# Hybrid decoder block: stick-breaking attention rebuilt around a scan from PSUM, weighing on POOL, and a transposed output

## The reference

```python
logits = q @ k.T * 64 ** -0.5
mask = key_pos[None, :] < q_pos[:, None]
log_1m_beta = where(mask, log_sigmoid(-logits), 0)
after = reverse_cumsum(log_1m_beta) - log_1m_beta
w = where(mask, exp(log_sigmoid(logits) + after), 0)
out = w @ v
```

## Time and profile before

| | us |
|---|---|
| Median of 3 runs | 3464.99 |
| All runs | 3459.66 to 3466.51 |
| Span of the profiled execution | 3462.9 |

### The profile page before, as it was taken

How to read it: one execution, slowest core, us unless ns; L and a number is a source line. 1 busy time by engine, 2 the same in 40 slices (tenths; PEclk the granted TensorE clock), 3 DMA queues, 4 the chain that set the end, 5 groups by cost and what they waited for, 6 DMA issues and landing times. The chain is left out here.

```text
span 3462.9 us, 45834 instructions
## 1 busy us (share of the span) xinstructions
PE 3115.5 (90%) x16210; PEld 2630.0 (76%) x16210; DVE 1877.4 (54%) x2584; ACT 1109.0 (32%) x1924; POOL 406.0 (12%) x245
## 2 busy tenths in 40 slices
PE   6999909978888896997699979999999899999998
PEld 5888807768778785886588758888888788888887
DVE  4332266579889896342666544444444544444444
ACT  4333205445555555231344321111111121111110
POOL 1221237612122121100000000000000000000000
PEclk9999959989999998998799989999999999999999
DMA  5233251062232203232422251111111311111111
GB/s 163 78 85 94 65 68 33 26 164 50 52 88 59 51 7 80 85 109 86 145 69 90 80 194 49 48 48 48 48 48 47 148 61 48 48 48 48 48 36 61
DMA packets 244273, 251.76 MB, mean 73 GB/s; under 512 B 123520, under 2 KB 197248, under 8 KB 244096
## 3 DMA queue, kind: packets, MB, share of 16 engines
q1 hardware_dynamic: 244112, 249.74, 24.7%
HBM read 189.79 MB, written 58.73 MB: 72 GB/s over the span
## 5 line engine op out<-in xcount | busy, mean ns | idle before, releaser
L2478 DVE TENSOR_TENSOR f_y<-f_ps_down,f_y 128x1024 f32<-128x1024 f32 x256 | 313.2, 1224 | 324.8 <-PE f_ps_down L2588 324.8
L2421 ACT ACTIVATE f_act_f<-f_ps_up 128x512 f32<-128x512 f32 x128 | 76.5, 598 | 1031.6 <-PE f_ps_up L2572 1031.6
L2570 PE MATMUL f_ps_up<-f_ht_hi,f_up_hi 128*128 128x512 f32 x1024 | 401.0, 392 | 6.4 <-DVE f_act_f L2495 6.4
L2586 PE MATMUL f_ps_down<-f_down_hi,f_a_hi 128*128 128x512 f32 x1024 | 400.5, 391 | 6.1 <-issue 6.1
L2571 PE MATMUL f_ps_up<-f_ht_lo,f_up_hi 128*128 128x512 f32 x1024 | 400.3, 391 | 0.0
L2572 PE MATMUL f_ps_up<-f_ht_hi,f_up_lo 128*128 128x512 f32 x1024 | 400.1, 391 | 0.0
L2588 PE MATMUL f_ps_down<-f_down_hi,f_a_lo 128*128 128x512 f32 x1024 | 400.1, 391 | 0.0
L2587 PE MATMUL f_ps_down<-f_down_lo,f_a_hi 128*128 128x512 f32 x1024 | 399.9, 390 | 0.0
L2495 DVE SCALAR_TENSOR_TENSOR f_act_f<-f_ps_up,f_act_f 128x512 f32<-128x512 f32 x128 | 88.5, 691 | 394.9 <-ACT f_act_f L2421 394.9
L823 PE MATMUL a_ps_y<-a_v,a_wt 128*128 128x64 f32 x2176 | 275.9, 277 | 0.0
L823 PEld LDWEIGHTS a_ps_y<-a_v,a_wt 128*128 128x128 f32 x2176 | 267.8, 196 | 1.7
(11 more groups left out here) (317 smaller groups left out, 5925.1 us busy)
## 6 DMA issues: line engine op xcount, KB each, us to landing
f_up_raw<-in_w_up SPq DMA_DIRECT2D x32, 1024.0 KB, 5.4
f_down_raw<-in_w_down SPq DMA_DIRECT2D x32, 1024.0 KB
p_xt<-in_x SPq DMA_DIRECT2D x16, 512.0 KB, 4.8
q<-p_qt SPq DMA_DIRECT2D x16, 512.0 KB, 3.2
k<-p_qt SPq DMA_DIRECT2D x16, 512.0 KB, 3.2
a_q<-q SPq DMA_DIRECT2D x16, 512.0 KB, 9.1
a_k_hi<-k SPq DMA_DIRECT2D x32, 256.0 KB, 5.7
a_k_lo<-k SPq DMA_DIRECT2D x32, 256.0 KB, 6.8
```

Source lines behind the costliest of these rows:

```text
L2478: dve.tensor_tensor(y[:, t, :], down_ps[t % 2][:, :], y[:, t, :], ALU.add).then_inc(added.sem, 1)
L2570: pe.matmul(o, up_hi[:, k, cols], ht_hi[:, k, rows], start=(k == 0), stop=False)
L2586: pe.matmul(o, a_hi[par][:, s, rows], down_hi[:, s, cols], start=(s == 0), stop=False)
```

## The change

- A step now interleaves its two heads: slots alternate between them, each head has its own `left` pair, and all 192 slots are written out with no loop; semaphores count straight through.
- ACT writes `on` first (to SBUF), then sigmoid(-z) in place in PSUM. DVE scans from PSUM, with a broadcast column of ones as the second operand. `off` is gone. A score now waits for the scan of the slot two before it.
- POOL weighs all slots.
- The copies of the transposed groups are shared so that every third group is DVE's, the others ACT's.
- The order: PE does turn(m - 2), gather(m - 6) for both heads at every second slot, score(m + 2); ACT the sigmoids of m, then the copies of m - 4; DVE scan(m), copies of m - 4, output copy of m - 8. There are three `on` and `w` and four `wt` buffers; `z_ps`, `wt_ps` and `y_ps` stay at two each.
- The gather has `v` stationary (64 columns) and `wt` moving (128 columns): head 0 writes partitions 0 to 63 of `y_ps`, head 1 the other half, so the output is transposed (`y_sb` becomes 512 x 2048) and is stored in rows of channels.
- Queries, keys and values come in halves of 1024 positions, keys and values with three buffers. A score piece ends at the half's edge.
- In `mix_heads` the transposes of `ys` are gone; `ys` and its squares live in the freed weight buffers. ACT squares and rounds all four tiles of a step, POOL adds the four tiles of squares of both halves together (four additions a step), and PE sums with 8 products instead of 16. `sums` and `norms` move from the end of a step to the start of the next, behind the first product.

The core of the diff:

```diff
+    SLOTS = [(s, a, *u) for s in range(STEPS) for u in UNITS for a in range(2)]
+    ONS, WS, WTS = 3, 3, 4
+    TURN_LAG, COPY_LAG, GATHER_LAG, Y_LAG = 2, 4, 6, 8
-        by_act = [g[1] > 0 or g[0] % 3 == 0 for g in groups]
+        by_act = [g % 3 != 2 for g in range(len(groups))]
...
+            def sigmoids(m):
+                z = z_ps[m % 2][:, 0:k1 - k0]
+                act.wait_ge(scored, m + 1)
+                if m >= ONS:
+                    act.wait_ge(weighed, m - ONS + 1)
+                act.activation(on[m % ONS][:, 0:k1 - k0], z, ACT.Sigmoid, scale=SCALE).then_inc(sig_on, 1)
+                act.activation(z, z, ACT.Sigmoid, scale=-SCALE).then_inc(sig_off, 1)
...
+            for m in range(N + COPY_LAG):
+                if m < N:
+                    sigmoids(m)
+                if m >= COPY_LAG:
+                    copies(m - COPY_LAG)
...
+                dve.tensor_tensor_scan(left[a][i % 2][:, at + k0:at + k1][:, ::-1], z_ps[m % 2][:, 0:k1 - k0][:, ::-1],
+                                       one[:, 0:1].to_broadcast([P, k1 - k0]),
+                                       1.0 if first else left[a][i % 2][:, at + k1:at + k1 + 1],
+                                       ALU.mult, ALU.bypass).then_inc(scanned, 1)
...
+            for m in range(N + Y_LAG):
+                if m < N:
+                    scan(m)
+                if COPY_LAG <= m < N + COPY_LAG:
+                    copies(m - COPY_LAG)
+                if m >= Y_LAG and m % 2 == 0:
+                    copy_y(m - Y_LAG)
...
+            def score(m):
+                if m >= 2:
+                    pe.wait_ge(scanned, m - 1)
...
+            def turn(m):
+                pe.wait_ge(weighed, m + 1)
+                for g in range(first_group[m], first_group[m + 1]):
+                    if g >= 2:
+                        wait_copied(pe, g - 2)
...
+            def gather(m):
+                wait_copied(pe, first_group[m + 2] - 1)
+                for t in range(tiles):
+                    for a in range(2):
+                        mm = pe.matmul(y_ps[i % 2][a * HEAD:(a + 1) * HEAD, 0:P], v[a][(2 * s + half) % 3][:, row, :],
+                                       wt[(m + a) % WTS][:, t, :], start=(first and t == 0), stop=(last and t == tiles - 1))
...
+            for m in range(N + GATHER_LAG):
+                if TURN_LAG <= m < N + TURN_LAG:
+                    turn(m - TURN_LAG)
+                if m >= GATHER_LAG and m % 2 == 0:
+                    gather(m - GATHER_LAG)
+                if m + 2 < N:
+                    score(m + 2)
...
+                pool.wait_ge(y2_squared.sem, y2_squared.at(c, NF))
+                pool.tensor_tensor(y2_sq[:, 0:2, :], y2_sq[:, 0:2, :], y2_sq[:, 2:4, :], ALU.add).then_inc(folded.sem, 1)
+                pool.wait_ge(ys_squared.sem, ys_squared.at(c, NF))
+                pool.tensor_tensor(ys_sq[:, 0:2, :], ys_sq[:, 0:2, :], ys_sq[:, 2:4, :], ALU.add).then_inc(folded.sem, 1)
...
-            def turn(c, j, count):
-                for k in range(4):
-                    mm = pe.transpose(turn_ps[:, k, :], ys[:, j, k * P:(k + 1) * P], ident[:, :])
```

More of the change, by code:

```diff
@@ L630, in wait_copied @@
[L630 to L645, removed]
+        q_loaded = [sem(f"q_loaded{h}") for h in range(2)]
@@ L647, in _, with wait, wait_copied, load_half @@
+        block = ctx.enter_context(nc.Block())
+        def wait(eng, of, count):
+            if count > 0:
+                eng.wait_ge(of, count)
+        def wait_copied(eng, g):
+            wait(eng, copied_a, acts_before[g + 1])
+            wait(eng, copied_d, g + 1 - acts_before[g + 1])
         @block.sync
         def _(sp):
[L649 to L653, removed]
+            def load_half(s, half):
+                cols = slice(half * HALF, (half + 1) * HALF)
+                r = (2 * s + half) % 3
@@ L717, in copies @@
                         _, t0, n = groups[g]
[L718 to L728 removed]
+                        act.wait_ge(turned, g + 1)
@@ L771, in _ @@
-            with dve.Fori(0, STEPS) as s:
-                for m in range(N + 4):
-                    if m < N:
-                        scan(s, m)
-                    if 1 <= m <= N and not by_pool[m - 1]:
-                        weigh(dve, s, m - 1, weighed)
-                    if 2 <= m < N + 2:
-                        copies(s, m - 2)
-                    if m >= 4:
-                        copy_y(s, m - 4)
+                    dve.wait_ge(gathered, m // 2 + 1)
+                    if s > 0:
+                        dve.wait_ge(y_stored[i // (BLOCKS // 2)], s * DMA)
@@ L802, in score @@
+                    mm = pe.matmul(out, q2[a][:, i * P:(i + 1) * P], k2_lo[a][r][:, cols], start=False, stop=closes and not diagonal)
                     if diagonal:
@@ L827, in _ @@
-            with pe.Fori(0, STEPS) as s:
-                score(s, 0)
-                score(s, 1)
-                for m in range(N + 3):
-                    if m + 2 < N:
-                        score(s, m + 2)
-                    if m >= 3:
-                        gather(s, m - 3)
-                    if 1 <= m <= N:
-                        turn(s, m - 1)
+                    mm.then_inc(turned, 1)
+            def gather(m):
+                s, _, i, k0, k1, first, last = SLOTS[m]
+                wait_copied(pe, first_group[m + 2] - 1)
+                if first:
+                    half = i // (BLOCKS // 2)
+                    if i in (0, BLOCKS // 2):
+                        pe.wait_ge(v_loaded[half], (s + 1) * 2 * DMA)
+                    wait(pe, y_copied, blocks_of[m] - 1)
+                tiles = (k1 - k0) // P
+                for t in range(tiles):
+                    tile = k0 // P + t
+                    half, row = tile // (BLOCKS // 2), tile % (BLOCKS // 2)
+                    for a in range(2):
+                        mm = pe.matmul(y_ps[i % 2][a * HEAD:(a + 1) * HEAD, 0:P], v[a][(2 * s + half) % 3][:, row, :],
+                                       wt[(m + a) % WTS][:, t, :], start=(first and t == 0), stop=(last and t == tiles - 1))
+                mm.then_inc(gathered, 1)
@@ L1443, in _ @@
                 first.load_weights(sp, n, w_loaded[n % RAW])
-            for j in range(TILES):
-                load_ys(0, j)
+            load_ys(0)
             load_uy(1)
```

380 lines of the change are left out of this document (172 added, 208 removed).

## The result

| | before | after |
|---|---|---|
| Median, us | 3464.3 (4 runs) | 4044.7 (4 runs) |
| All runs | 3459.7 to 3466.5 | 4041.3 to 4050.6 |
| Ratio, 95% interval | | 1.168 [1.166, 1.170] |
| Attention in the profiled execution | 697 to 1343 | 697 to 1932 |
| From attention's end to the last instruction | 2120 | 2116 |

The forecast was 4130 with a range of 3930 to 4310, and rival 3 (the two heads' gathers side by side) said 4045. Attention takes 1235 us instead of 646, and nothing else changed by more than 4 us.

What follows compares the result with a forecast made beforehand. Attention was taken as throughput-bound, DVE first, until the new order makes PE's score wait on older copies: 3463 + 684 (attention) - 17 (mixing) = 4130, 4132 with 2 us to the median, given as 4130; range 3930 to 4310, own range 4030 to 4230.

Steps and rivals of the forecast that it cites:

- rival 3: Attention's gather: two heads' products run side by side in PE's array, 0.06 us per record; total 4045 us; chance 0.16.
- What bounded before, and the engines' gains: Attention: throughput binds, DVE first; DVE falls from 561 to about 400 us, POOL gets 394, ACT stays near 400.
- The wait that the new order makes: PE's queue: score(m + 2) waits for slot m + 1's sigmoids and DVE-group scan; none ahead for 160 of 192 slots.
- One turn: Attention's chain from score to next score: 6.63 us mean, 7.8 with the clock, for each of 160 slots.
- The gather: PE in attention: 0.09 us per record, since the load is half as wide; 1.13 us per slot, ends 0.76 and 1.47.
- The clock: PE in attention: idle gaps lower the granted clock, half the work at each level, adding 1.2 us per turn.
- Mixing: After attention: fewer transposes and sums on PE, about 1 us of POOL's additions showing; -17 us, bounds -25 and +10.
- 1: PE's clock in attention stays high despite the idle gaps; total 3943 us; chance 0.13.
- 2: PE's clock in attention stays low nearly throughout; total 4338 us; chance 0.13.
- 4: Attention: transposes do not hold the score, the two `z_ps` tiles bind at 2.5 us a slot; total 3286; chance 0.05.
- What would show it: Attention's profile: PE, DVE, ACT each under half busy, hardly any overlap, clock near 0.7; wrong if attention under 1000 us.
- -160 us: Attention: what it would lose from DVE's lighter work if throughput still bound; the new order was to prevent it.

Runs made afterwards that it cites:

- e1: Changed kernel with PE's order score(m+2), gather(m-6), turn(m-2) instead of turn, gather, score: 3357.1 us, ratio 0.970 to the kernel before.
- e2: Changed kernel, its order on PE kept, with copies 3 slots behind instead of 4: 3458.5 us (1 run).
- e4: Changed kernel with the gather's loops exchanged, all tiles of head 0 and then of head 1: 4115.6 us (1 run).
- e6: Changed kernel with PE's order score, gather, turn and the gather's loops exchanged, one head after the other: 3396.8 us, ratio 0.980 to the kernel before.
- e10: Kernel before with scan from PSUM, all weighing on POOL, copies 3 slots behind instead of 2, gather 4 instead of 3: 3451.6 us, ratio 0.995.
- e13: Kernel before with scan from PSUM, all weighing on POOL, later copies and gather, and output copied 6 slots behind instead of 5: 3454.4 us, ratio 0.996.
- e9: Kernel before with only POOL weighing every slot, the scan still reading SBUF: 3485.8 us (1 run).
- e8: Kernel before, old order, with only the second sigmoid kept in PSUM for the scan and POOL weighing every slot: 3532.8 us, ratio 1.020.

## Why the prediction was right

**What bounded before, and the engines' gains.** DVE 390 us of attention (about 400 forecast), scans 324 (319), ACT 372 (near 400): right. POOL 283, not 394: I scaled its 2.05 us of the earlier trace rows, measured beside scans that read SBUF; 768 columns take 1.55, apart from any scan in the changed kernel and beside scans from PSUM in e1. That nothing of this shows in the time was right, for the reason given.

**The wait that the new order makes.** Shown, by e1 and e2 against the changed kernel: place and lag of the score cost 688 us, more than the 589 by which attention grew, since the other parts gain about 100 once the ring is open. The count of slots was the step that carried the prediction. One detail of it is off: a slot of exactly four tiles has one group, and each head has two such slots (one is half of the nine-tile block), so 152 slots have two groups and 40 have one, not 160 and 32. From scan to scan the changed kernel's trace gives the 152 slots 1028 us, 6.8 each, and the small ones, priced at 2 us, 165 us, 4.2 each. So the turn was overestimated by more, and the small slots underestimated, than the division below shows; it keeps the forecast's counts, to be laid beside its terms.

**One turn.** With the forecast's 64 + 12 + 5 us for small slots and ends, the measured turn is (1235 - 81) / 160 = 7.2 us; forecast 7.8. Term by term:

- Sigmoids (0.81 + 0.81 for 768 columns) and scan (1.76 to 1.82 for 768): as forecast. The sigmoid of 768 columns that writes PSUM takes 0.81 us, as much as the one that writes SBUF.
- ACT's end to the scan: forecast 0.28 from one row, measured 1000.02 + 1.02 to 1001.07, 0.03, which is also the median of all 192. For the two thirds of slots with a DVE group: -27 us.
- The gather: forecast 0.09 at the high clock, 0.129 with my clock; measured 0.107. On 160 x 6.3 x 4 / 2 = 2016 records -45 us. This is the term that was mis-sized most. Its mechanism was wrong too: the forecast let a narrower load make every record faster, and e4 and e6 show that the pairing of the two heads does (unpaired, e6's products start every 0.109 us, against 0.112 in the kernel before, whose load is twice as wide). e4, without the pairing, takes 4116 against my 4130, but that is no confirmation: its record takes 338.3 / 2176 = 0.155 us, not 0.129.
- The clock: half at each level would be 0.75, "near 0.7" was written, measured 0.65. The factor between the levels, 0.42 / 0.23 us, is 1.83 and not 1.87.
- Mixing: 13 us less gained than forecast.

Together -59 of the -85 us; the rest lies in the transposes, the small slots and the start (the first product comes 19 us into attention, where 12 were allowed), and I did not separate it. In the forecast's own range the lower end of the gather is -85 us by the working that gives +78, not -75; so 4045 was inside the range of the forecast as well as being rival 3's time, and the time alone could not tell the two apart.

**The rivals.** 1 and 2 (clock high, clock low throughout) are answered by the granted 0.65; that the clock has no size of its own apart from the ring was not tried, since a filler for PE's gaps would have needed a PSUM bank of its own. 3 had the right mechanism, by e4 and e6; that its time came out to the microsecond is luck. Its gather record, 0.06 x 1.43 = 0.086 us, was measured at 0.107 (+42 us), mixing gained 13 less, the hand-over to the scan took 27 off, and some 28 more went with the terms that I did not separate. 4 is near what e1 shows when the ring is open: 547 us instead of its 485. Even there the transposes wait 65 us for copies, and the first product comes only 18 us into attention; which of them makes the difference was not tried.

**What would show it.** Right: waits, order of the rows, scans of 768 columns at 1.76 to 1.82 us (though hardly any of them beside POOL in this kernel), no attention under 1000. Wrong: PE was to be under half busy, and was 714 of 1235, 58%. My own sum (2.7 + 1.2 of 7.8) gave half.

**Where "-160 us" stood on weak ground.** I took the engine gains as real but unused. With the ring open, e1 takes 99 us off attention, not 160, and that with the gather's gain in it. In the old order, with the old gather, e10 and e13 show the engine gains worth 9 to 16 us. e1, with the new order and gather, is 107 us faster than before, and e6, with the new order and the gather unpaired, 67; so the pairing is worth 40 of it, and what the rest owes to the interleaved heads, the narrower gather or the loop written out was not separated.

## What to carry to other kernels

Where a loop is written out as one queue per engine, count for each instruction that all others wait for (here the score) how many slots its queue's predecessors lag behind, through every engine: if the count is zero the pipeline is a ring, whatever the engines' load. Changing a buffer's release (the scan instead of the sigmoid frees PSUM) moves that count, so the lags have to be counted again; one line's place was worth 688 us here. And price a part only with its partners: POOL's weighing alone (e9) gained nothing (22 us slower in its one run), with the scan from PSUM but the old lag (e8) it lost 69 us; with the longer lag as well (e10) the same parts gained 16, and in the new order, with the new gather (e1), 107.

## What the hardware showed that I had not expected

- Two heads' products that write partitions 0 to 63 and 64 to 127 in turn run side by side, in pairs that start 6 ns apart: 32 in 1.97 us, against 3.33 when one head follows the other.
- POOL's weighing of 768 columns takes 1.55 us beside scans that read PSUM (e1) and 2.26 beside scans that read SBUF (e9); those scans take 1.76 to 1.81 and 2.42 to 3.11.
- Longer PE work inside the ring went with a higher clock and cost less than its own length (0.65 to 0.71; 106 us more of gather, 71 more in all; e4 ran once).
- DVE's skips in mixing, 0.69 us each alone, take 1.43 beside POOL's folds (5.72 for four), and its `TENSOR_SCALAR` on 128x8, 0.17 us alone, 1.05 to 1.22 beside POOL.
